# Two-model block on one core: double expert loads from chunk 42 of a layer, and three of the last norm's four gain products on GpSimd

## The reference

```python
def first_block(x, ...):
    for layer in range(2):
        m = conv_mixer(x, ...) if layer == 0 else rglru_mixer(x, ...)
        x = layer_norm(ALPHA * x + m, ln1_g[layer], ln1_b[layer])
        f = moe(x, w_router, b_router, w1[layer], w3[layer], w2[layer])
        x = layer_norm(ALPHA * x + f, ln2_g[layer], ln2_b[layer])
    return x

def moe(...):   # per token the best two of one group's four experts, 16 experts in all
    hb = silu(xb @ w1[e]) * (xb @ w3[e]);  y = hb @ w2[e]

def second_block(x, ...):   # layer 0: forgetting attention, layer 1: dilated attention
    for layer in range(2):
        x = x + mixer(...)
        x = x + conv_ffn(rms_norm(x, ffn_norm_g[layer]), ...)
    return rms_norm(x, final_norm_g)      # x * rsqrt(mean(x*x) + 1e-6) * g
```

## Time and profile before

| | us |
|---|---|
| median of three runs | 1774.01 |
| lowest, highest | 1773.5, 1775.23 |
| the profiled execution, its own time | 1775.5 |
| span from its first to its last instruction | 1774.2 |
| PE busy | 1709.8 (96%) |
| DVE busy | 791.5 (45%) |
| ACT busy | 625.2 (35%) |
| POOL busy | 122.4 (7%) |
| loads of 2 MB from the w tensors into ring, early, F, ZX | 100, 16, 16, 8 |

### The profile page before, as it was taken

One profiled execution on the slowest core, in us unless ns is written; L12 is line 12 of the kernel. 1 busy time (PEld: TensorE's weight loads), 2 busy tenths in 40 slices (PEclk: granted clock), 3 DMA queues, 4 the chain that ended last, 5 costly groups with the idle time before them and its releaser, 6 DMA issues.

```text
span 1774.2 us, 23971 instructions
## 1 busy us (share of the span) xinstructions
PE 1709.8 (96%) x9996; PEld 1116.9 (63%) x9996; DVE 791.5 (45%) x1522; ACT 625.2 (35%) x1201; POOL 122.4 (7%) x145
## 2 busy tenths in 40 slices
PE   9999999999989989999999989999999999999998
PEld 8974344433334974444343333887999898789986
DVE  6961111111103782111111012866888677668875
ACT  5541111000002661100000002666666564756664
POOL 0000000000000000000000000131111001401100
PEclk9999999999999999999999999999999999999999
DMA  9769999999999789999999999434555544335550
GB/s 387 314 232 381 387 428 428 428 430 426 426 426 419 284 320 395 423 429 429 429 426 429 425 426 419 174 129 143 177 180 190 190 167 149 137 131 178 179 190 24
DMA packets 55971, 544.88 MB, mean 307 GB/s; under 512 B 6320, under 2 KB 6320, under 8 KB 8368
## 3 DMA queue, kind: packets, MB, share of 16 engines
q1 hardware_dynamic: 55440, 542.14, 75.8%
q10 hardware_dynamic: 416, 1.13, 0.2%
HBM read 542.19 MB, written 1.05 MB: 306 GB/s over the span
## 4 chain that ended last, share of the span: by engine, by line
PE 71%; DMA 16%; DVE 7%; ACT 3%; issue 1%; POOL 1%; SPq 0%; ACTq 0%; DVEq 0%
PE PS L1231 24%; DMA ring<-in_w 16%; PE PS L421 12%; PE PS L423 11%; PE PS L422 11%; PE PS L1213 2%; PE PS L1285 2%; DVE wl L404 2%; PE PS L1431 2%; PE PS L950 1%; PE PS L1247 1%; ACT wh L398 1%; PE PS L1299 1%; PE PS L1404 0%; DVE sm L593 0%
## 5 line engine op out<-in xcount | busy, mean ns | idle before, releaser
L1231 PE MATMUL PS<-ring,F 128*64 128x512 f32 x1992 | 447.4, 598 | 27.5 <-DMA ring<-in_w 23.4
L404 DVE TENSOR_TENSOR wl<-ring,wh 128x512 fp32r<-128x512 f32 x504 | 362.4, 737 | 167.4 <-ACT wh L398 164.9
L398 ACT ACTIVATE wh<-ring 128x512 fp32r<-128x512 f32 x504 | 314.5, 630 | 270.0 <-PE PS L423 251.9
L1231 PEld LDWEIGHTS PS<-ring,F 128*64 128x64 f32 x1992 | 142.3, 138 | 312.0 <-issue 273.6
L421 PE MATMUL PS<-xh,wl 128*128 128x256 f32 x1144 | 329.8, 288 | 2.7 <-DVE wl L404 2.6
L422 PE MATMUL PS<-xl,wh 128*128 128x256 f32 x1144 | 323.6, 283 | 0.0
L423 PE MATMUL PS<-xh,wh 128*128 128x256 f32 x1144 | 323.5, 283 | 0.0
L421 PEld LDWEIGHTS PS<-xh,wl 128*128 128x128 f32 x1144 | 219.2, 192 | 5.8 <-DVE wl L404 2.7
L422 PEld LDWEIGHTS PS<-xl,wh 128*128 128x128 f32 x1144 | 219.3, 192 | 0.7
L423 PEld LDWEIGHTS PS<-xh,wh 128*128 128x128 f32 x1144 | 219.3, 192 | 0.0
L421 PE MATMUL PS<-wh,xl 128*128 128x512 f32 x352 | 142.6, 405 | 6.5 <-DVE xl L566 3.4
(11 more groups left out here) (422 smaller groups left out, 1907.5 us busy)
## 6 DMA issues: line engine op xcount, KB each, us to landing
ring<-in_w SPq DMA_DIRECT2D x100, 2048.0 KB, 25.6
ring<-in_w SPq DMA_DIRECT2D x65, 1024.0 KB, 11.7
ring<-in_ffn_up SPq DMA_DIRECT2D x44, 1024.0 KB, 4.9
early<-in_w SPq DMA_DIRECT2D x16, 2048.0 KB, 26.6
F<-in_w SPq DMA_DIRECT2D x16, 2048.0 KB, 27.9
ring<-in_ffn_down SPq DMA_DIRECT2D x22, 1024.0 KB, 4.9
F<-in_w SPq DMA_DIRECT2D x20, 1024.0 KB, 9.3
ZX<-in_w SPq DMA_DIRECT2D x8, 2048.0 KB, 28.0
```

Of the source, the lines that this page charges most:

```text
L398: act.e.activation(self.wh[:, p % NPIECE, :], self.piece_source(p), ACT.Copy).then_inc(*self.up("w_hi", p))
L404: dve.e.tensor_tensor(self.wl[:, p % NPIECE, :], self.piece_source(p), f32(self.wh[:, p % NPIECE, :]), ALU.subtract).then_inc(*self.up("w_ ...
L1231: t = pe.e.matmul(PS[64 * half:64 * half + 64, bank, :], lhs(k), weights[:, a:a + 512], start=(k == 0), stop=(k == 7))
```

## The change

Two independent edits. The first: loads of two chunks begin with chunk 42 of an expert layer, so chunks 40 and 41 are loaded one at a time. The table of slots is worked out anew from that. In layer 0 chunk 40 now goes to slot 16, behind chunk 9, and chunk 41 to slot 21, behind chunk 10, where the pair had waited for chunks 20 and 21; the pair 42, 43 waits for 20 and 21 (before: 22 and 23), 44, 45 for 22 and 23 (24 and 25), 46, 47 for 24 and 25 (26 and 27), 48, 49 for 26 and 27 (10 and 28), and from chunk 50 on the chunks waited for are the same but for 62, 63 and 180. In layer 1 chunk 40 waits for chunk 9 alone and 41 for chunk 10, where the pair had waited for 9 and 11; the pairs 128 to 139 wait for chunks 2 to 10 numbers later than before (128, 129 for 112 and 113, before 106 and 107); and the first two dense chunks behind the layer, `aq0` 0 and 1, wait for chunks 185 and 186, before for 179 and 181.

The second: in the last stage ACT puts its squares into scratch columns of F, does all four squares before its two scalings, and three of the four products by the norm's weights are done by POOL (`pool_gain`), the fourth by DVE. `ffn_pool` of layer 0 of the second model keeps its order.

```diff
 def _load_size(i):
-    return 2 if 40 <= i < 180 else 1
+    return 2 if 42 <= i < 180 else 1
...
-            act.e.activation(self.Z[:, h, c], self.X[:, h, c], ACT.Square, scale=1.0 / 32,
+            squares = self.F[:, 8704 + 512 * d:9216 + 512 * d] if stage == "down1" else self.Z[:, h, c]
+            act.e.activation(squares, self.X[:, h, c], ACT.Square, scale=1.0 / 32,
...
-        self.scalar_rms(stage, stage, 0)
-        self.scalar_finish(0)
-        self.scalar_rms(stage, stage, 1)
-        self.scalar_finish(1)
+        for h in range(2):
+            self.scalar_rms(stage, stage, h)
+        for h in range(2):
+            self.scalar_finish(h)
...
-        for h in range(2):
-            self.pool_rstd(h, (f"down{layer}", h))
+        if layer:
+            for d in range(2):
+                self.pool_gain(0, d)
+        self.pool_rstd(0, (f"down{layer}", 0))
+        if layer:
+            self.pool_gain(1, 0)
+        self.pool_rstd(1, (f"down{layer}", 1))
...
-        self.vector_residual("down1", p, nk, 0, 1.0, self.X)
-        self.vector_rms_sum("down1", 0)
-        gain(0, 0)
-        gain(0, 1)
-        self.vector_residual("down1", p, nk, 1, 1.0, self.X, halves=(0,))
-        scale(0)
-        self.vector_residual("down1", p, nk, 1, 1.0, self.X, halves=(1,))
-        gain(1, 0)
-        self.vector_rms_sum("down1", 1)
-        gain(1, 1)
-        scale(1)
+        self.vector_residual("down1", p, nk, 0, 1.0, self.X)
+        self.vector_rms_sum("down1", 0)
+        self.vector_residual("down1", p, nk, 1, 1.0, self.X)
+        dve.wait_ge((self.s_row, 48), at("resid", "down1", 1, 1))
+        dve.e.tensor_tensor(self.Z[:, 1, 512:1024], self.X[:, 1, 512:1024], self.last_gain()[:, 512:1024], ALU.mult
+                            ).then_inc(*up("y_gain_last"))
+        self.vector_rms_sum("down1", 1)
+        for h in range(2):
+            dve.wait_ge(at("rstd", ("down1", h)), at("y_gain_last") if h else at("y_gain", 0, 1))
+            dve.e.tensor_scalar(self.Z[:, h, 512:1024], self.Z[:, h, 512:1024], self.sm[:, 500 + h:501 + h], None,
+                                ALU.mult).then_inc(*up("y_ready1", h))
+
+    def pool_gain(self, h, d):
+
+        c = slice(d * 512, d * 512 + 512)
+        self.pool.wait_ge((self.s_row, 48), self.at("resid", "down1", h, d))
+        self.pool.e.tensor_tensor(self.Z[:, h, c], self.X[:, h, c], self.last_gain()[:, c], ALU.mult).then_inc(
+            *self.up("y_gain", h, d))
```

More of the change, by code:

```diff
@@ L2972, in vector_finish, with last_gain @@
         dve, at, up = self.dve, self.at, self.up
[L2973 to L2981, removed]
+        self.vector_residual("down1", p, nk, 0, 1.0, self.X)
[7 more added lines that the diff above has]
+            dve.wait_ge(at("rstd", ("down1", h)), at("y_gain_last") if h else at("y_gain", 0, 1))
             dve.e.tensor_scalar(self.Z[:, h, 512:1024], self.Z[:, h, 512:1024], self.sm[:, 500 + h:501 + h], None,
                                 ALU.mult).then_inc(*up("y_ready1", h))
-        self.vector_residual("down1", p, nk, 0, 1.0, self.X)
-        self.vector_rms_sum("down1", 0)
-        gain(0, 0)
-        gain(0, 1)
-        self.vector_residual("down1", p, nk, 1, 1.0, self.X, halves=(0,))
-        scale(0)
-        self.vector_residual("down1", p, nk, 1, 1.0, self.X, halves=(1,))
-        gain(1, 0)
-        self.vector_rms_sum("down1", 1)
-        gain(1, 1)
-        scale(1)
+    def last_gain(self):
+        return self.F[:, 12288:13312]
+    def pool_gain(self, h, d):
[3 more added lines that the diff above has]
+            *self.up("y_gain", h, d))
     def scalar_finish(self, h):
```

## The result

| us | before | changed |
|---|---|---|
| median | 1774.45 | 1769.97 |
| lowest, highest (11 runs each) | 1773.37, 1775.46 | 1768.17, 1771.42 |
| the profiled execution, its own time | 1775.5 | 1769.29 |
| its span | 1774.2 | 1768.0 |

The changed kernel is 4.5 us faster: ratio 0.9975, 95% interval 0.9967 to 0.9983. That is inside the predicted range of 1767.2 to 1771.7 and 1.0 us above the predicted time, of which 0.4 us is the median of before (1774.45 here, 1774.01 when I predicted). The two spans differ by 6.2 us, more than the medians do, because single executions scatter by 2 to 3 us.

What follows compares the result with a forecast made beforehand. The prediction took the DMA queue to bound the expert layers, with one hole in layer 0, and a chain on DVE to bound the tail. 1774.0 - 3.9 - 1.1 gave 1769.0 us, range 1767.2 to 1771.7.

Steps and rivals of the forecast that it cites:

- Edit 1, layer 0: Earlier loads of chunks 40 and 41 fill the DMA hole at 177 to 183 us: -3.9 us.
- the chain of waits: In layer 0 it runs through TensorE's products up to 348 us, then a load from 356.47 landing after 44.5 us.
- the mean of the engines: Layer 0's hole priced by the engines' mean idle share from 177 to 183 us: 4.2 us.
- the slowest landing: Layer 0's hole priced by chunks 40 and 41 landing at 185.5 instead of 189.2: 3.7 us.
- the lower bound of 1.4: Least gain in layer 0: only the slowest engine's own idle time, about 180 to 181.4 us, counts.
- Edit 1, layer 1: Longer waits of pairs 128 to 139 and the first two dense loads are covered by the queue: cost 0.
- Edit 2: In the tail DVE adds the last block earlier, so the last scaling starts at 1769.7 instead of 1770.82: -1.1 us.
- The sum: Whole kernel: -3.9 - 1.1 = -5.0 us, from a median of 1774.0 to 1769.0 us.
- rival 1: Layer 0: only the slowest engine counts, so 1.4 us are won there; 1771.5 us, chance 0.12.
- rival 3: Layer 0's hole is not on the path, so only the tail gains; 1772.9 us, chance 0.06.
- rival 4: Layer 1's later waits drain the queue, up to +10.2 us; 1779.2 us, chance 0.02.
- rival 2: GpSimd becomes the bound of the tail, last scaling 0.2 us later than now; 1770.3 us, chance 0.10.

Runs made afterwards that it cites:

- half_hole: The changed kernel, but the load of chunk 40 of layer 0 also waits for chunk 20: 1771.81 us, ratio 0.9986.
- tail_only: The changed kernel with the loads of before (double loads from chunk 40), so only the tail is changed: 1773.08 us, ratio 0.9994.
- layer0_only: The kernel before, with double loads from chunk 42 in layer 0 only; layer 1 and tail as before: 1770.46 us, ratio 0.9978.
- give_up_104: The changed kernel, but in layer 1 the slots beside the ring are given up at load 104 instead of 128: 1770.61 us, ratio 0.9977.
- pool_two: The changed kernel with only half 0's two products on GpSimd, DVE doing the third and fourth: one profiled execution, 1768.91 us.
- pool_four: The changed kernel with the fourth product on GpSimd too, ahead of the second power: one profiled execution, 1769.34 us.
- loads_only: The kernel before, with double loads from chunk 42 in both expert layers and the tail unchanged: 1770.96 us, ratio 0.9981.
- from_44: The changed kernel with double loads from chunk 44 instead of 42: 1769.55 us, ratio 0.9975.

## Why the prediction was right

- **Edit 1, layer 0: -3.9 predicted, -3.8 measured** (mean layer lengths; -3.1 to -3.7 as medians of the whole). The step that carried it was not to take the chain of waits at face value: a load that lands 44.5 us after its issue stands in a queue, so what sets its landing is where the queue last ran dry. The chain's own piece then shrank by 4.2 us. The two middle values, the mean of the engines (4.2) and the slowest landing (3.7), lie too close together for the lengths to choose between them; the lower bound of 1.4 is excluded. The Trainium skill's rule (DMA: Bandwidth & Descriptors, "Why a DMA increments its semaphore by 16 and not by 1") that only the full 16 means landed is true of each load, and the traces agree: in before, fifteen engines were done with chunk 39 by 178.9 us and the last at 180.5, which is its landing. Taken as a price for the hole the rule would have given the 3.7 or the 1.4, as the prediction says. The 3.7 fits. The 1.4, for which only the late engine's own idle time counts, doesn't: half_hole and tail_only speak against it.
- **What I had slightly off there.** I took the next landings from the slowest engine, which was to stay late: chunk 41 at 185.5 and the pair 42, 43 behind it at 185.5 + 4.9 = 190.4. They landed at 183.8 and 189.6. No engine of the changed kernel was as late under chunk 39 as one was in before (landing 11.6 us after issue instead of 13.0). How late the last engine is differs from one execution to the next.
- **Edit 1, layer 1: 0 predicted, none seen** beyond the scatter, with the layer0_only and give_up_104 kernels behind it. The cover was the queue of some 36 us. The added wait took some 9 us of it (41.6 to 32.2 from issue to landing), about the 10 of the prediction, and even a queue of 14 us (18.8 less the 4.9 of the transfer) does.
- **Edit 2: -1.1 predicted, -1.2 in the trace** (4.24 to 3.01 us; 7.64 to 6.48 to the end of the span), -1.0 as a median. The cover held: the third product ended 0.7 us before the power was asked for, predicted 0.4. The size of the power was the unknown; I took 0.93 and it was 0.72, between the bounds of 0.55 and 0.93. The difference was partly taken back by DVE, whose product took 0.84 us instead of the 0.68 that I reckoned with: its sum starts 1.97 us after the last matmul here and at 1.90 in pool_two, where no product of POOL overlaps it. The Trainium skill's advice to keep elementwise work on VectorE (GPSIMD Engine Reference, "Engine selection") is right about the price, 1.27 to 1.30 us against 0.68 here, and would have decided wrongly: with GpSimd idle, the three products cost the end no more than that 0.07 us. What the new order of DVE and ACT would have gained with all four products left on DVE, no run shows; of the moves to GpSimd only the third (pool_two) and the fourth (pool_four) were tried one by one.
- **The sum.** -5.0 predicted and -4.5 measured. The two edits alone add to -4.1 by medians and to -5.0 by the traces' stretches (3.8 and 1.2), so the 0.5 us is within what medians of 11 runs scatter (1.4 us to either side). **Rivals** 1, 3 and 4 each met a run that speaks against them: half_hole, loads_only, give_up_104. Against rival 2 speaks the changed kernel itself, where POOL waits 0.75 us for the sum before the power; pool_four shows the case in which it would have held. Its sum in the prediction was wrong: three products of 1.70 and two powers of 0.93 from 1763.7 on end at 1770.7, not at 1771.0, so its time was 1770.0 instead of 1770.3. Nothing else hangs on it.

What stays open is the scatter of a layer's length. Layer 1 with the same loads took 422.8 to 424.4 us, and layer 0 of from_44 was 1.8 us longer than that of the changed kernel though its median was no slower. Single DMA engines were up to 2.7 us behind most of the others, but I haven't shown that they cause it.

## What to carry to other kernels

In a stage whose DMA queue is full, ask when it was last empty, not who waits: a chain of waits that runs through TensorE and ends in a load with a landing time many times its own transfer can hide a hole that lies far earlier (170 us here). Price the hole by the mean idle share of the 16 engines times its length, and test it by putting the wait back. In a tail, take off the engine that receives the last block everything that doesn't need that block, even onto an engine that is twice as slow, if that engine is idle and done before it is next asked. The second part rests on the tail as a whole; its reordering was not tried by itself.

## What the runs showed of the hardware

- GpSimd's power of 128 x 1 takes 0.55 us beside an idle DVE, 0.72 beside DVE's scaling of one SBUF block (one SBUF block in, one out), and 0.93 to 0.95 beside DVE's product of two SBUF blocks. It took 0.55 as well where DVE's residual, which has one of its inputs in PSUM, ran beside half of it (the changed kernel's power at 1761.24). The Trainium skill says of this (GPSIMD Engine Reference, "Specifications") that the two share SBUF interfaces and contend when DVE has two SBUF inputs or runs in a 2-port mode. The 0.95 bears out the first; the 0.72 would be the second if the scaling runs in such a mode, which no run here shows.
- It goes the other way too, which I hadn't expected: DVE's product took 0.84 us instead of 0.68 while POOL ended its third product (0.68 in pool_two, where POOL had none then), and DVE's scaling 0.98 instead of 0.47 while POOL multiplied (pool_four).
- Loads of 2 MB moved 428 GB/s and loads of 1 MB 422 in the same stretch, both with the engines full. I had reckoned with more: I expected 11 to 12 us for giving up the double loads and measured 8.4.
